# Attention masks moved from TensorE products into the key biases

## The reference

```python
# branch A (forgetting attention), F = cumsum(log_sigmoid(fa + forget_b))
s = einsum('bqhd,bkhd->bhqk', qb, k) * scale + Fq[..., None] - F_k[:, :, None, :]
s = where(k_pos <= q_pos, s, NEG_INF)              # causal
# branch B (chunks of 64; every chunk sees its own and the 8 before it)
s = einsum('bnqhd,bnkhd->bnhqk', qc, k_band) * scale + bias   # rel_bias[clip(t - s)]
s = where(key_valid, s, NEG_INF)
# both
p = softmax(s); out = einsum(p, v)
```

## Time and profile before

| what | value |
|---|---|
| time, median of 3 runs (lowest, highest) | 1219.64 us (1219.07, 1219.81) |
| span of the profiled execution | 1215.5 us (its profile gives no time of its own beside it) |
| TensorE busy, weight loads busy | 1170.6 us (96%), 956.1 us (79%) |
| VectorE, ScalarE, GpSimd busy | 623.0 us (51%), 476.6 us (39%), 18.9 us (2%) |
| mean granted TensorE clock | 0.981 |
| DMA | 147.91 MB, mean 122 GB/s |

### The profile page before, as it was taken

How to read it: one execution, slowest core, us unless ns; L and a number is a source line. 1 busy time by engine, 2 the same in 40 slices (tenths; PEclk the granted TensorE clock), 3 DMA queues, 4 the chain that set the end, 5 groups by cost and what they waited for, 6 DMA issues and landing times.

```text
span 1215.5 us, 15501 instructions
## 1 busy us (share of the span) xinstructions
PE 1170.6 (96%) x5320; PEld 956.1 (79%) x5320; DVE 623.0 (51%) x1019; ACT 476.6 (39%) x709; POOL 18.9 (2%) x34
## 2 busy tenths in 40 slices
PE   5899999999999989999999999997999999999997
PEld 4788888888788767888878888785888888888885
DVE  3776665765444466655555666746333333333332
ACT  4232323232222265555555655524344443422222
POOL 0000000000000000000000000000000000000000
PEclk9699999999999989999999999998999999999999
DMA  9556556556444313333343332231333333323332
GB/s 319 167 174 204 193 164 225 168 185 189 146 147 147 99 35 105 87 88 87 120 127 84 87 86 70 87 104 35 104 104 93 97 100 89 104 83 94 95 95 82
DMA packets 221588, 147.91 MB, mean 122 GB/s; under 512 B 5333, under 2 KB 207204, under 8 KB 221556
## 3 DMA queue, kind: packets, MB, share of 16 engines
q1 hardware_dynamic: 216772, 139.02, 38.2%
q0 software_dynamic: 2672, 6.39, 1.6%
q10 hardware_dynamic: 2112, 2.10, 0.5%
HBM read 145.32 MB, written 4.25 MB: 123 GB/s over the span
## 4 chain that ended last, share of the span: by engine, by line
PE 60%; issue 32%; DVE 3%; DMA 2%; ACT 2%; POOL 0%; ACTq 0%; DVEq 0%; POOLq 0%; SPq 0%
PE bank L1075 17%; PE bank L1077 17%; PE bank L1076 17%; PE bank L1241 1%; PE bank L1228 1%; DMA adas<-in_ada_w_dram 1%; DMA raw<-in_mix_w_in_dram 1%; PE bank L1234 1%; PE bank L1257 1%; PE bank L1256 1%; ACT wH L464 1%; DVE adasc L767 1%; PE bank L1329 1%; DVE wL L680 0%; DMA bias<-negF_d 0%
## 5 line engine op out<-in xcount | busy, mean ns | idle before, releaser
L1075 PE MATMUL bank<-hH,wH 128*128 128x512 f32 x1096 | 434.6, 397 | 11.8 <-DVE hL L755 9.0
L1076 PE MATMUL bank<-hL,wH 128*128 128x512 f32 x1096 | 430.1, 392 | 0.0
L1077 PE MATMUL bank<-hH,wL 128*128 128x512 f32 x1096 | 429.8, 392 | 0.0
L464 ACT ACTIVATE wH<-raw 128x1024 fp32r<-128x1024 f32 (+1 forms) x193 | 201.0, 1042 | 551.6 <-PE bank L1077 540.7
L680 DVE TENSOR_TENSOR wL<-raw,wH 128x1024 fp32r<-128x1024 f32 (+1 forms) x193 | 231.9, 1202 | 335.6 <-ACT wH L464 334.9
L1075 PEld LDWEIGHTS bank<-hH,wH 128*128 128x128 f32 x1096 | 207.8, 190 | 60.1 <-issue 9.8
L1077 PEld LDWEIGHTS bank<-hH,wL 128*128 128x128 f32 x1096 | 207.7, 189 | 43.9
L1076 PEld LDWEIGHTS bank<-hL,wH 128*128 128x128 f32 x1096 | 207.9, 190 | 42.0
L1075 PE MATMUL bank<-actH,wH 128*128 128x512 f32 x352 | 139.1, 395 | 0.0
L1076 PE MATMUL bank<-actL,wH 128*128 128x512 f32 x352 | 139.0, 395 | 0.0
L1077 PE MATMUL bank<-actH,wL 128*128 128x512 f32 x352 | 139.0, 395 | 0.0
(11 more groups left out here) (148 smaller groups left out, 865.9 us busy)
## 6 DMA issues: line engine op xcount, KB each, us to landing
raw<-in_ffn_w_gate_dram SPq DMA_DIRECT2D x44, 512.0 KB, 3.8
raw<-in_ffn_w_up_dram SPq DMA_DIRECT2D x44, 512.0 KB, 3.8
adaw<-in_ada_w_dram SPq DMA_DIRECT2D x22, 1024.0 KB, 6.1
raw<-in_mix_w_in_dram SPq DMA_DIRECT2D x41, 512.0 KB, 3.8
raw<-in_ffn_w_down_dram SPq DMA_DIRECT2D x32, 512.0 KB, 3.7
adas<-in_ada_w_dram SPq DMA_DIRECT2D x12, 512.0 KB, 9.2
adaw<-in_ada_w_dram SPq DMA_DIRECT2D x8, 768.0 KB, 4.9
raw<-in_ffn_w_down_dram SPq DMA_DIRECT2D x16, 384.0 KB, 3.3
```

Of the source, the lines that this page charges most:

```text
L464: nc.scalar.activation(wH[s][:, :n * P], raw[s][:, :n * P], ACT.Copy).then_inc(hi_done, 1)
L1075: T.matmul(o, a[0], b[0], start=start, stop=False)
L1076: T.matmul(o, a[0], b[1], start=False, stop=False)
L1077: return T.matmul(o, a[1], b[0], start=False, stop=stop)
```

## The change

TensorE no longer multiplies `identb` by `mask`; both tiles and the work that made them are gone. In branch A GpSimd loads the biases of each pass in four DMAs, one for each query tile, into a new tile `biasA` laid out as the scores are (2 heads x 1280 columns). When all four have landed it puts NEG_INF into the masked part of each tile's last square with an `affine_select` (2 x 128 columns each), and VectorE waits for all four selects. In branch B GpSimd overwrites, in DRAM, the last 64 columns of the first 64 rows of each head in `relb_d` with NEG_INF, once, by one more DMA from a new tile `negm`, before the first read of `relb_d`.

```diff
             pool.wait_ge(consts_v, 3)
...
-            nc.gpsimd.affine_select(out=mask[0][:, :], in_=mask[0][:, :], ...).then_inc(masks_made, 1)
+            def pair_biases_a():
+                pool.wait_ge(negF_out, 16)
+                for i in range(PAIRS):
+                    pool.wait_ge(biased, i * 8 + START)
+                    for t in T_ORDER:
+                        w = P * (t + 1)
+                        pool.dma_start(biasA[:, :, T_OFF[t]:T_OFF[t] + w],
+                                       negF_d[2 * i:2 * i + 2, 0:w].partition_broadcast(P)).then_inc(biasA_in, 16)
+                    pool.wait_ge(biasA_in, i * (16 * TT) + 16 * TT)
+                    for t in T_ORDER:
+                        own = biasA[:, :, T_OFF[t] + P * t:T_OFF[t] + P * (t + 1)]
+                        nc.gpsimd.affine_select(out=own, in_=own, compare_op=ALU.is_ge, fill=NEG_INF, base=0,
+                                                pattern=[[0, 2], [-1, P]], channel_multiplier=1).then_inc(biasA_masked, 1)
...
                     pool.dma_start(negF_d, fgate[:, 5, :]).then_inc(negF_out, 16)
-                    pair_biases(0)
+                    nc.gpsimd.memset(negm[:, :, :], NEG_INF).then_inc(negm_made, 1)
+                    pair_biases_a()
...
                     pool.dma_start(relb_d, bass.AP(relx_d.tensor, ...)).then_inc(relb_out, 16)
-                    pair_biases(1)
+                    pool.wait_ge(relb_out, 16)
+                    pool.wait_ge(negm_made, 1)
+                    pool.dma_start(relb_d.rearrange("h p s -> p h s")[0:P // 2, :, SEQ - P // 2:], negm[:, :, :]).then_inc(relb_masked, 16)
+                    pair_biases_b()
...
-                                if n == 0:
-                                    dve.wait_ge(bias_in, g * 16 + 16)
+                                if n == 0 and br == 0:
+                                    dve.wait_ge(biasA_masked, i * (2 * TT) + (TT * pp + TT))
+                                elif n == 0:
+                                    dve.wait_ge(bias_in, i * 32 + (16 * pp + 16))
...
-            V.memset(mask[0][:, :], 0.0).then_inc(consts_v, 1)
-            V.memset(mask[1][:, :], 0.0).then_inc(consts_v, 1)
...
-            V.memset(mask[1][0:64, 64:P], NEG_INF).then_inc(masks_made, 1)
-            V.tensor_copy(identb[:, :], ident[:, :]).then_inc(identb_made, 1)
...
                                     T.matmul(o, qHH[:, hh, cols], kHL[:, hh, :w], start=True, stop=False)
-                                    T.matmul(o[:, w - P:], identb[:, :], mask[br][:, :], start=False, stop=False)
```

More of the change, by code:

```diff
@@ L115, in hybrid_block @@
         ident = sb("ident", [P, P])
-        identb = sb("identb", [P, P], BF16)
-        mask = [sb(f"mask{b}", [P, P], BF16) for b in range(2)]
         ones = sb("ones", [P, P])
@@ L179, in hybrid_block @@
             relx = sb("relx", [HB, SEQ + P], stack=in_mix)
+            biasA = sb("biasA", [P, 2, CW], stack=in_mix)
+            negm = sb("negm", [P // 2, HB, P // 2], stack=in_mix)
         modrow = tmp[0:1, 0, :]
@@ L264, in hybrid_block @@
         bias_in = sem("bias_in")
+        biasA_in = sem("biasA_in")
+        biasA_masked = sem("biasA_masked")
+        negm_made = sem("negm_made")
+        relb_masked = sem("relb_masked")
         qhi = sem("qhi")
@@ L406, in _, with pair_biases_b @@
         def _(pool):
-            pool.wait_ge(consts_v, 5)
+            pool.wait_ge(consts_v, 3)
             nc.gpsimd.affine_select(out=ident[:, :], in_=ident[:, :], compare_op=ALU.not_equal, fill=1.0, base=0,
                                     pattern=[[-1, P]], channel_multiplier=1).then_inc(ident_made, 1)
[L411 to L414, removed]
-                with pool.Fori(0, PAIRS) as i:
[L417 to L421, removed]
+            def pair_biases_a():
[11 more added lines that the diff above has]
+                                                pattern=[[0, 2], [-1, P]], channel_multiplier=1).then_inc(biasA_masked, 1)
+            def pair_biases_b():
+                pool.wait_ge(relb_masked, 16)
+                with pool.Fori(0, PAIRS) as i:
+                    pool.wait_ge(biased, i * 8 + 8 * PAIRS + START)
+                    src = relb_d.rearrange("h p s -> p h s")[:, ds(i * 2, 2), :]
                     pool.dma_start(bias[:, :, :], src).then_inc(bias_in, 16)
@@ L909, in biased_scores @@
                                 w = P * (t + 1)
-                                b0 = (0, SEQ - w)[br]
-                                if n == 0:
-                                    dve.wait_ge(bias_in, g * 16 + 16)
+                                if n == 0 and br == 0:
+                                    dve.wait_ge(biasA_masked, i * (2 * TT) + (TT * pp + TT))
+                                elif n == 0:
+                                    dve.wait_ge(bias_in, i * 32 + (16 * pp + 16))
+                                if br == 0:
+                                    key_bias = biasA[:, h, T_OFF[t]:T_OFF[t] + w]
+                                else:
+                                    key_bias = bias[:, h, SEQ - w:]
                                 wait_apart(s_done, g * 8 + (h + (1, 5, 5, 7)[n]) + START, spare[:, 4 * h + n:4 * h + n + 1])
@@ L918, in biased_scores @@
                                     in0=bank[:, S_BANK[h]:S_BANK[h] + 3, :].rearrange("p a b -> p (a b)")[:, T_OFF[t]:T_OFF[t] + w],
-                                    in1=bias[:, h, b0:b0 + w], scale=-1.0, scalar=BIG, op0=ALU.add, op1=ALU.min,
+                                    in1=key_bias, scale=-1.0, scalar=BIG, op0=ALU.add, op1=ALU.min,
                                     accum_out=negmax[:, h, t:t + 1]).then_inc(biased, 1)
@@ L1004, in _ @@
             V.memset(ident[:, :], 0.0).then_inc(consts_v, 1)
-            V.memset(mask[0][:, :], 0.0).then_inc(consts_v, 1)
-            V.memset(mask[1][:, :], 0.0).then_inc(consts_v, 1)
             V.memset(ones[:, :], 1.0).then_inc(consts_v, 1)
             V.memset(mhalf[:, :], -0.5).then_inc(consts_v, 1)
-            dve.wait_ge(consts_v, 3)
-            V.memset(mask[1][0:64, 64:P], NEG_INF).then_inc(masks_made, 1)
-            dve.wait_ge(consts_v, 4)
+            dve.wait_ge(consts_v, 2)
             V.tensor_copy(onesr[:, :], ones[:, 0:2]).then_inc(onesr_made, 1)
-            dve.wait_ge(ident_made, 1)
-            V.tensor_copy(identb[:, :], ident[:, :]).then_inc(identb_made, 1)
             dve.wait_ge(c_act, 1)
@@ L1341, in _ @@
             two_units(U_FA, (B_FA, 0), DT)
-            pe.wait_ge(identb_made, 1)
-            pe.wait_ge(masks_made, 2)
             pairs(0)
```

2 lines of the change are left out of this document (removed).

## The result

The changed kernel takes 1223.19 us (median of 6 runs, 1221.27 to 1224.69) against 1219.22 us (6 runs, 1216.75 to 1219.81). The ratio is 1.0038, 95% interval 1.0027 to 1.0048: slower by 0.4%. Timed once more, later, it was 1.0027 (1.0016 to 1.0039), with a median of 1222.97 us.

What follows compares the result with a forecast made beforehand. TensorE, busy 96% of the span, was taken to set the pace in seven of eight passes, the first hanging on the biases' arrival. Terms +4.9 + 1.9 - 5.6 = +1.2 us on 1219.6 gave 1220.8 us, range 1216.0 to 1223.8.

Steps and rivals of the forecast that it cites:

- the sum of +1.2 us: Whole kernel: first-bias delay +4.9, halved clock +1.9, removed products -5.6, giving 1220.8 us.
- the delay of the first `turn(0)`: First pass of branch A: late biases push the first transposes back 4.9 us, paid in full.
- The saving, 5.6: Mask products gone from TensorE: 0.8 us less in each of seven passes, 5.6 us (5.0 to 7.8).
- the gap of 0.10: Tile t = 3: 0.10 us beside the second mask belongs to switching 128-row to 64-row stationaries, and stays.
- The delay of the first biases, 4.9: First pass, branch A: four DMAs landing at 466.9, then selects of 1.6 us, start VectorE 4.9 us later (2.1 to 6.8).
- the prediction's even share: First bias loads: added 0.79 MB sharing DMA engines evenly with weight loads takes 4.4 us; 3.3 was chosen.
- What hangs behind it is the whole chain: First pass behind VectorE's start: biased scores, exponentials, `p_ready`, `turn(0)` all shift; nothing hides the 4.9 us.
- The clock, 1.9: After a 7.3 us TensorE stall before the first `turn(0)`: half clock for 3.7 us, costing 1.9 us.
- Branch B and the other passes, 0: Branch A's passes 2 to 4 hide loads and selects; branch B's biases come 6 us later, hidden: 0.
- (a): Rival: the 0.10 gap goes with the masks (7.8 saved), biases delayed only 3.0, clock holds: 1214.8 us; chance 23%.
- (c): Rival inside the forecast's class: the stall doesn't throttle the clock, rest as forecast, -0.7 us: 1218.9; no separate chance.
- (b): Rival: first biases later still through DMA queueing and dear selects, +6.8, deciding from 6.1: 1223.3 us; chance 25%.

Runs made afterwards that it cites:

- experiment 1: Kernel before without the mask products, so nothing is masked: 1215.12 us, ratio 0.9969.
- experiment 3: Branch B as in the changed kernel, branch A with one load and mask products as in the kernel before: 1214.50 us, ratio 0.9971.
- experiment 8: Changed kernel, but branch A's first pass has one bias load and mask products as before: 1211.96 us, ratio 0.9941.
- experiment 12: Kernel before without mask products (nothing masked), plus 8 idle products ahead of unit 3 in the first pass: ratio 0.9959.
- experiment 4: Changed kernel without branch A's four selects per pass, so branch A is unmasked and VectorE waits for the loads alone: 1219.78 us, ratio 1.0004.
- experiment 5: Changed kernel with branch A's four loads cut to 2 x 128 columns each, other key biases left zero: 1221.39 us, ratio 1.0019.
- experiment 11: Kernel before with branch A's four bias loads written out instead of looped, masks still by TensorE: ratio 0.9992.
- experiment 6: Changed kernel plus 34 idle 512-column products ahead of unit 3 in the first pass, filling TensorE's stall: 1221.12 us, ratio 1.0018.
- experiment 7: Changed kernel with one semaphore per tile's load in branch A, selects and biased scores following tile by tile: 1218.80 us, ratio 0.9992.
- experiment 2: Changed kernel with the mask products put back, so entries are masked twice: 1227.36 us, ratio 1.0072.
- experiment 9: Changed kernel timed again with no edit, beside the kernel before: 1222.97 us, ratio 1.0027.

## Why the prediction was wrong

It forecast no measurable change, 1220.8; the range held the 1223.19, but the kernel is measurably slower: the interval of the ratio is 0.1% to either side, where the prediction had thought 0.2% to be the limit of what can be told. Most of its mechanisms were there; the sum of +1.2 us was too small, and the term that failed is the delay of the first `turn(0)`, forecast as 4.9 us and measured as 6.0.

- **The saving, 5.6.** Measured 7 x 0.77 = 5.4. The reading of the rows by start-to-start distances and the choice to leave the gap of 0.10 in place were right. Shown by the tile in the changed kernel (0.98 us, forecast 1.00), and by experiments 1, 3, 8 and 12.
- **The delay of the first biases, 4.9: the step that failed, by its size.** VectorE started 5.5 us later against the first scores and `turn(0)` 6.0. The loads cost 3.8 instead of 3.3, the selects 1.7 instead of 1.6 (experiment 4). The 3.8 hides two errors. From their first issue the loads took 4.4 us longer than the one before, the prediction's even share and not the 3.3 that it chose. And the first issue came 0.6 us earlier, because the change wrote out the loop, which the prediction put at nothing without a word. The prediction put the loads down to the bytes; experiment 5 shows that the bytes account for 1.6 us, and that the rest stays with four loads of the old one's bytes: 2.2 against the kernel before. Against experiment 11, which has one load written out and VectorE's start 5.39 us behind the first scores, the four loads cost 10.70 - 5.39 = 5.3 us, so that rest is 3.7.
- **What it had not counted: VectorE itself, 0.5.** "What hangs behind it is the whole chain" was priced as a pure shift. But `turn(0)` came 5.4 us behind VectorE's start instead of 4.96. The four normalisations of head 0 took 1.74 us instead of 1.27, while GpSimd was issuing the next pass's four loads (474.57 to 477.54). In the second pass it is the same, 1.74, in branch B, with one load, 1.38; in the kernel before all are 1.27. But the overlap alone doesn't make it: in the first pass of experiment 6 the issues begin at the same 0.17 us behind the normalisations and these take 1.27, and experiments 4 and 7 have 1.29 and 1.27, while 2, 5 and 9 have 1.73 or 1.74. Where they take 1.27, `turn(0)` comes 4.96 us behind VectorE's start again (476.14 - 471.18 in experiment 6). What decides it stays open. The Trainium skill (GPSIMD Engine Reference, Specifications) says that GpSimd shares its SBUF interfaces with VectorE and that some VectorE instructions contend for them; that would fit the 1.74 and leaves the 1.27 unexplained.
- **The clock, 1.9.** Measured 2.1, and shown by experiment 6, in which the first transposes start at the same time and only the clock differs behind them. The wait was 8.3 us, not 7.3. Half clock lasted 4.4 us behind the first transpose instead of 3.7. The price varies from profile to profile: behind the first transpose experiments 2, 4, 5, 7 and 9 lose 1.7, 2.8, 1.4, 2.1 and 2.0 us.
- **Branch B and the other passes, 0.** Right (experiments 2 and 3). The added load held up branch B's biases by 3.5 us (617.02 to 620.51), not 6, and all of it was hidden.
- **The rivals.** (a), the gap belongs to the mask: refuted. (c), the clock holds: refuted. (b) came nearest: it decides "from a delay of 6.1", and the delay was 6.0. Half of its mechanism was there: the loads took the 4.4 us more that it gave them, the selects were not dear (1.7 of its 2.4 us). That its 1223.3 almost equals the measured 1223.19 is luck: the stages add up to 1222.

The sum with the measured terms is +6.0 + 2.1 - 5.4 = +2.7 us, 1222. By the ratios, the two timings of the changed kernel say 4.6 and 3.3 us. The rest, 0.6 to 1.9 us, is not settled. Both stretches outside the change differ between profiles of one kernel by as much, so it may be chance; it was not traced to an edit. The stages of the other kernels, added up in the same way, fall within the intervals of their ratios, but for experiments 5 and 6, which are slower than their stages by 1.9 and 1.5 us.

## What to carry to other kernels

Work moved off the bound engine is paid where its replacement is first needed: look up the one pass in which the operand was already late, and keep the old way there. Here that is 7.2 us faster than the kernel before, where the change applied everywhere is 3 to 5 us slower. By the stages the masks are worth 5.4 of it and writing out a loop of loads 1.5, which the kernel before could have had by itself. So look through an edit for what it changes besides its purpose. Price a stall of TensorE with the clock behind it, and look at waits that already exist: removing 0.8 us of products in front of a wait of 1.5 us cost 1.6 us of clock in the one profile taken.

## What the runs showed of the hardware

- The granted clock was halved at the end of a wait of 2.3 us (experiment 1), and not by one of 1.5 (kernel before) or of 0.5 (experiments 6 and 12). Yet a wait of 3.01 us ahead of the second FFN left it full in the kernel before and halved it in the changed one. So the length alone doesn't decide. The Trainium skill (TensorE: Matmul & The Clock Gate, The HAM clock gate) says that idleness throttles the array; that so short a wait can do it is experiment 1's, with experiment 12 as its check.
- Between a product with a 128-row stationary and one with a 64-row stationary stands a gap of 0.08 to 0.10 us, with and without a bf16 product in between.
- A GpSimd select of 2 x 128 float32 columns takes 0.37 to 0.41 us. The Trainium skill (GPSIMD Engine Reference, Performance versus the Vector engine) gives 1.8 cycles per element at best at 1.2 GHz, an estimate of 0.38 us for 256 elements. That match isn't worth much: for 128 the same estimate is 0.19, and the trace has 0.29. From the recorded 0.29 to 0.40 us, 128 more columns cost 0.11.
- A loop around GpSimd's first load cost 0.6 us of issue and 1.5 us until its data was used (experiment 11; 6.59 us from the write of `negF_d` to VectorE's start instead of 8.06).
